# Dilated attention with plain f32 queries and keys, double-buffered loads, and both attentions' first loads moved ahead

## The reference

```python
DIL_GROUPS = ((128, 1), (512, 4), (2048, 16))
for g in range(G):
    idx = t[:, None] - offsets[g][None, :]
    kg, vg = k_groups[g][:, idx], v_groups[g][:, idx]
    logits = jnp.einsum('bqhd,bqkhd->bhqk', qb[:, :, g], kg) * scale + group_bias[g]
    logits = jnp.where(valid, logits, NEG_INF)
    lse = jax.nn.logsumexp(logits, axis=-1)
    outs.append(einsum('bhqk,bqkhd->bqhd', jnp.exp(logits - lse[..., None]), vg)); lses.append(lse)
wts = softmax(stack(lses)); return einsum('gbhq,gbqhd->bqhd', wts, stack(outs))
```

## Time and profile before

| | |
|---|---|
| Runs | 3153.85, 3158.89, 3159.69 us, median 3158.89 |
| Profiled execution | 3164.19 us, of which the span of the trace is 3162.4 us |
| Granted TensorE clock, mean | 0.964 |
| Busy | PE 2896.8 us (92%), PEld 2372.0, DVE 1163.2, ACT 858.4, POOL 923.8 |
| Chain that ended last | PE 81%, DVE 8%, DMA 4%, issue 3%, ACT 2% |
| QK<-y_odds, loads | 128 of 256 KB |
| Packets under 512 bytes | 26211 of 91069 |

### The profile page before, as it was taken

The page is one execution under the profiler, slowest core; times in us unless marked ns, Lnnn a source line. Parts: engine busy times, 40 slices in busy tenths (PEclk is TensorE's granted clock), DMA queues, the critical chain, the costliest instruction groups (busy, mean ns, idle before and its releaser), DMA issues.

```text
span 3162.4 us, 36743 instructions
## 1 busy us (share of the span) xinstructions
PE 2896.8 (92%) x13588; PEld 2372.0 (75%) x13588; DVE 1163.2 (37%) x1849; ACT 858.4 (27%) x1489; POOL 923.8 (29%) x610
## 2 busy tenths in 40 slices
PE   8996888889999999999999975767889999999998
PEld 5785777767888888886788865657668888888867
DVE  3425777414222222225423133467252222222254
ACT  3304766423110001025210024456340000011141
POOL 2330145342333333342233201122413333333332
PEclk9998999999999999999999986879999999999999
DMA  4336432211111111111235267764211111111111
GB/s 153 129 115 180 121 86 68 74 47 34 47 49 50 46 46 46 53 54 54 80 127 215 74 163 137 109 153 114 83 35 47 47 47 52 46 46 46 67 34 73
DMA packets 91069, 257.03 MB, mean 81 GB/s; under 512 B 26211, under 2 KB 29795, under 8 KB 90647
## 3 DMA queue, kind: packets, MB, share of 16 engines
q1 hardware_dynamic: 76008, 199.74, 22.8%
q10 hardware_dynamic: 14944, 55.74, 4.6%
HBM read 207.24 MB, written 52.93 MB: 82 GB/s over the span
## 4 chain that ended last, share of the span: by engine, by line
PE 81%; DVE 8%; DMA 4%; issue 3%; ACT 2%; SPq 1%; POOL 1%; DVEq 0%; ACTq 0%; POOLq 0%
PE ACC L1097 68%; PE ACC L1243 4%; PE OP L1280 3%; PE TR L1257 3%; DMA QK<-y_odds 2%; PE OP L1167 2%; DVE XL L1723 1%; DVE PT L1880 1%; DVE H L1743 1%; DVE T L1740 1%; SPq L725 1%; ACT PT L1517 1%; DVE PB L1863 1%; PE OP L1270 1%; DVE XF L1914 1%
## 5 line engine op out<-in xcount | busy, mean ns | idle before, releaser
L928 POOL CAST WH<-RAW 128x1024 fp32r<-128x1024 f32 x203 | 213.7, 1053 | 1552.2 <-PE ACC L1097 1532.8
L1097 PE MATMUL ACC<-XH,WH 128*128 128x512 f32 x1792 | 574.3, 402 | 47.8 <-DVE XL L1723 27.1
L1097 PE MATMUL ACC<-XL,WH 128*128 128x512 f32 x1792 | 557.1, 392 | 0.0
L1097 PE MATMUL ACC<-XH,WL 128*128 128x512 f32 x1792 | 556.2, 392 | 0.0
L930 POOL TENSOR_TENSOR WL<-RAW,WH 128x1024 fp32r<-128x1024 f32 x203 | 490.5, 2416 | 24.8 <-POOL WH L928 1.5
L1097 PEld LDWEIGHTS ACC<-XH,WH 128*128 128x128 f32 x1792 | 337.4, 189 | 147.1 <-issue 65.4
L1097 PEld LDWEIGHTS ACC<-XL,WH 128*128 128x128 f32 x1792 | 339.7, 190 | 71.9
L1097 PEld LDWEIGHTS ACC<-XH,WL 128*128 128x128 f32 x1792 | 339.2, 189 | 71.8
L1478 ACT ACTIVATE HH<-T 128x1024 fp32r<-128x1024 f32 x64 | 68.0, 1062 | 1149.9 <-DVE T L1765 1149.9
L1772 DVE TENSOR_TENSOR M<-M,ACC 128x1024 f32<-128x1024 f32 x128 | 156.3, 1221 | 482.8 <-PE ACC L1097 480.6
L1097 PE MATMUL ACC<-HH,WH 128*128 128x512 f32 x1024 | 316.7, 390 | 3.3 <-DVE M L1772 3.1
(11 more groups left out here) (197 smaller groups left out, 3288.6 us busy)
## 6 DMA issues: line engine op xcount, KB each, us to landing
RAW<-in_w SPq DMA_DIRECT2D x203, 512.0 KB, 3.4
QK<-y_odds SPq DMA_DIRECT2D x128, 256.0 KB, 6.4
y_odds<-HALVES ACTq DMA_DIRECT2D x16, 1024.0 KB, 5.2
QK<-y_foxs SPq DMA_DIRECT2D x48, 256.0 KB, 5.4
y_foxs<-HALVES ACTq DMA_DIRECT2D x8, 1024.0 KB, 5.1
y_kv<-Q ACTq DMA_DIRECT2D x8, 512.0 KB, 2.6
BIAS<-y_f SPq DMA_DIRECT2D x8, 512.0 KB, 7.0
H<-in_xT ACTq DMA_DIRECT2D x8, 512.0 KB, 7.5
```

The costliest lines, as they stand in the source:

```text
L928: nc.gpsimd.tensor_copy(WH[:, slot], RAW[:, slot]).then_inc(s_whi, 1)
L1097: mm = nc.tensor.matmul(acc[:, h * HALF:(h + 1) * HALF], w(k), x[:, k, h * HALF:(h + 1) * HALF], start=first and k == k0 and w is ws and x ...
```

## The change

Queries and keys of the dilated groups are stored plain (y_odd, 20 tiles; those of the NSA and fox jobs stay split). A dilated job loads queries and keys of both heads as they are into QF (two places, by the job's number modulo 2), with one load of both biases; all its loads are issued by `dilated_loads` as soon as the job before has turned its V and the job two back that used the place is scored. A logit is one plain f32 product over the 64 rows of its head. The minima and sums of a d1 job are turned on PE (32 columns of NML to 32 rows), copied to ZT and stored in pieces of 512 bytes; the merge works on 32 partitions by 32 tokens. CQH and CQL move so that QK is free during up0. SP issues the first fox job's RV and QK before up0's weights, and the first dilated job's RV, QF and BIAS before in1c's weights.

```diff
@@ -69,9 +69,9 @@
-    segs.append(("in1p", 1, [full("odds", 0, 0, "x1"), full("odds", 1, 0, "x1"), full("odd", 6, 0, "x1"),
+    segs.append(("in1p", 1, [full("odd", 8, 0, "x1"), full("odd", 9, 0, "x1"), full("odd", 6, 0, "x1"),
                              full("odd", 7, 0, "x1")]))
-    segs.append(("in1a", 5, [full("odds", c, 2, "x1") for c in (2, 3)]))
+    segs.append(("in1a", 5, [full("odd", 8 + c, 2, "x1") for c in (2, 3)]))
     segs.append(("in1b", 3, [full("odd", c, 2, "x1") for c in (0, 1)]))
@@ -275,13 +275,17 @@
             j.before = jobs[-1] if jobs else None
+            same = [x for x in jobs if x.kind in DILATED and x.slot == j.slot] if kind in DILATED else []
+            j.same, j.loads = same[-1] if same else None, len(same) + 1
+            stacked = [x for x in jobs if x.kind in NSA]
+            j.stacked = stacked[-1] if stacked else None
             jobs.append(j)
@@ -432,8 +438,9 @@
         CQ = sb("CQ", [P, 3, S], 96)
-        CQH = sb("CQH", [P, 3, S], 108, F32R)
-        CQL = sb("CQL", [P, 3, S], 120, F32R)
+        CQH = sb("CQH", [P, 3, S], 0, F32R)
+        CKVL = sb("CKVL", [P, 1, S], 12, F32R)
+        CQL = sb("CQL", [P, 2, S], 16, F32R)
         MISC1 = sb("MISC", [P, 1, S], 132)
@@ -455,6 +462,7 @@
         RK = sb("RK", [P, S], 76)
+        QF = [sb("QF0", [P, 2, S], 8), sb("QF1", [P, 2, S], 180)]
         QK = sb("QK", [P, 2, 4, S], 96, F32R)
@@ -718,39 +739,71 @@
+            def load(dst, src, signal):
+                sp.dma_start(dst, src).then_inc(signal, 16)
+            def head_loads(j, e):
+                y = y_foxs if j.kind == "fox" else y_odds
+                q = y[j.pair + (12 if j.kind in NSA else 0)]
+                for half in range(2):
+                    load(QK[rows_of_head(half), e, 0].bitcast(F32), q[1 - half, rows_of_head(e)], s_head[e])
+                for r in range(2 if j.kind != "cmp" else 0):
+                    for half in range(2):
+                        if j.kind in ("sel", "win"):
+                            src = y[14 if j.kind == "sel" else 15, 1 - half, 0:HD]
+                        else:
+                            src = y[j.pair + (4), 1 - half, rows_of_head(e)]
+                        load(QK[rows_of_head(r), e, 2 + half].bitcast(F32), src, s_head[e])
+            def dilated_loads(j, prior=None):
+                g = j.pair + 2 * DILATED.index(j.kind)
+                if prior:
+                    sp.wait_ge(s_tr, prior.vgroups[-1].tr)
+                load(RV[:], y_odd[g], s_load)
+                if j.same:
+                    sp.wait_ge(s_ttr, j.same.tasks[-1].no + 1)
+                load(QF[j.slot][:, 0], y_odd[8 + g], s_dj[j.slot])
+                load(QF[j.slot][:, 1], y_odd[14 + g], s_dj[j.slot])
+                w = D16_W if j.kind == "d16" else DIL_W
+                load(BIAS[:, :, 256 * j.slot:256 * j.slot + w],
+                     b_tile[j.kind][2 * j.pair:2 * j.pair + 2].rearrange("h p w -> p h w"), s_dj[j.slot])
             def attention(name):
...
-                def load(dst, src, signal):
-                    sp.dma_start(dst, src).then_inc(signal, 16)
                 def sums_out(j):
...
-                    g = DILATED.index(j.kind)
+                    g, c0 = DILATED.index(j.kind), j.tasks[0].col
+                    if j.kind == "d1":
+                        sp.wait_ge(s_zc, j.pair + 1)
+                        sp.dma_start(z_sums[j.pair, g].rearrange("m e (i p) -> (m e i) p", p=P), ZT[:])\
+                            .then_inc(s_zs[g], 16)
+                        return
                     sp.wait_ge(s_exp, j.tasks[-1].no + 1)
...
                         for e in range(2):
-                            c0 = j.tasks[NB * e].col
-                            src, dst = NML[:, m, c0:c0 + NB], z_sums[j.pair, g, m, e]
-                            if j.kind == "d1":
-                                dst = dst.rearrange("(i p) -> p i", p=P)
-                            elif j.kind == "d4":
+                            src, dst = (minima, row_sums)[m](c0 + NB * e, NB), z_sums[j.pair, g, m, e]
+                            if j.kind == "d4":
                                 src = src.rearrange("p (b a) -> p b a", b=2)
...
                                 dst = dst.rearrange("(p i) -> p i", i=NB)
-                            sp.dma_start(dst, src, allow_slow_non_contiguous=j.kind == "d1").then_inc(s_zs[g], 16)
+                            sp.dma_start(dst, src).then_inc(s_zs[g], 16)
@@ -760,6 +813,18 @@
                     before = j.before if j is not ph.jobs[0] else None
+                    if j.kind in DILATED:
+                        if before:
+                            dilated_loads(j, before if before.vgroups else before.before)
+                        if before and before.kind in DILATED:
+                            sums_out(before)
+                        last_bias = j
+                        continue
+                    if j.kind == "mla" and j.pair == 0:
+                        last = tiles[seg_end["up0"] - 1]
+                        sp.wait_ge(s_store[0], 16 * last.store[0])
+                        sp.wait_ge(s_store[1], 16 * last.store[1])
                     if j.vgroups:
@@ -788,22 +851,13 @@
-                        if before:
-                            sp.wait_ge(s_qk, before.tasks[NB * e + NB - 1].no + 1)
-                        g = 2 * DILATED.index(j.kind) if j.kind in DILATED else 0
-                        y = y_foxs if j.kind == "fox" else y_odds
-                        q = y[j.pair + (12 if j.kind in NSA else g)]
-                        for half in range(2):
-                            load(QK[rows_of_head(half), e, 0].bitcast(F32), q[1 - half, rows_of_head(e)], s_head[e])
+                        user = j.stacked if j.kind in NSA else before
+                        if user:
+                            sp.wait_ge(s_qk, user.tasks[NB * e + NB - 1].no + 1)
+                        if before or name != "even":
+                            head_loads(j, e)
                         if j.kind == "cmp":
                             continue
-                        for r in range(2):
-                            for half in range(2):
-                                if j.kind in ("sel", "win"):
-                                    src = y[14 if j.kind == "sel" else 15, 1 - half, 0:HD]
-                                else:
-                                    src = y[j.pair + (4 if j.kind == "fox" else 6 + g), 1 - half, rows_of_head(e)]
-                                load(QK[rows_of_head(r), e, 2 + half].bitcast(F32), src, s_head[e])
@@ -846,17 +900,19 @@
             skew("d16", 8, D16_W)
-            for name in ("in0p", "in0b", "in0c", "up0"):
+            for name in ("in0p", "in0b", "in0c"):
                 weights(name)
...
-            last = tiles[seg_end["up0"] - 1]
-            sp.wait_ge(s_store[0], 16 * last.store[0])
-            sp.wait_ge(s_store[1], 16 * last.store[1])
+            for t in (segs["in0b"].iters[1][0].tiles[0], segs["in0c"].iters[0][0].tiles[0]):
+                sp.wait_ge(s_store[t.pair], 16 * t.store[t.pair])
+            sp.wait_ge(s_x, applies["cq"] + 3)
+            job = phases["even"].jobs[0]
+            load(RV[:], y_fox[0], s_load)
+            for e in range(2):
+                head_loads(job, e)
+            weights("up0")
+            sp.wait_ge(s_tile, segs["up0"].iters[0][1].tiles_end)
             sp.wait_ge(s_misc, 32)
-            sp.wait_ge(s_tile, seg_end["up0"])
-            sp.wait_ge(s_evD, tiles[seg_end["up0"] - 1].dve)
             attention("even")
@@ -881,6 +937,12 @@
             weights("in1b")
+            job = phases["odd"].jobs[0]
+            for t in (segs["in1p"].iters[0][0].tiles[0], segs["in1a"].iters[2][0].tiles[0], segs["in1b"].iters[0][0].tiles[0]):
+                sp.wait_ge(s_store[t.pair], 16 * t.store[t.pair])
+            sp.wait_ge(s_hsp, 16 * DC)
+            sp.wait_ge(s_bd, 16 * 6)
+            dilated_loads(job)
             weights("in1c")
@@ -889,9 +951,6 @@
             sp.wait_ge(s_vst, 32)
-            sp.wait_ge(s_hsp, 16 * DC)
-            sp.wait_ge(s_bd, 16 * 6)
             sp.dma_start(CMPMASK[:], ins["cmpmask"]).then_inc(s_bd, 16)
@@ -1225,6 +1284,14 @@
                     wait(pe, s_ttr, t.acc_free)
+                    if kind in DILATED:
+                        if t.first_of_head and e == 0:
+                            pe.wait_ge(s_dj[t.job.slot], 48 * t.job.loads)
+                        rows = rows_of_head(e)
+                        q, k = (QF[t.job.slot][rows, m, token(kind, b0):token(kind, b0) + c * (n - 1) + 1:c]
+                                for m, b0, n in ((0, t.i, P), (1, t.blocks[0], w)))
+                        nc.tensor.matmul(score_bank(t), q, k, start=True, stop=True).then_inc(s_qk, 1)
+                        return
                     if t.first_of_head and kind == "mla":
@@ -1257,6 +1324,11 @@
                         tr.then_inc(s_tr, 1)
```

(27 more changed lines are left out.)

57 lines of the change are left out of this document (31 added, 26 removed).

## The result

The changed kernel takes 3172.35 us (median of 5 runs, 3166.57 to 3175.32), the kernel before 3155.44 us (5 runs, 3151.96 to 3159.69): ratio 1.0045, 95% interval 1.0031 to 1.0059. It is slower by 17 us; 3094 us was forecast, and the range ended at 3116.

The account below looks back on a forecast made before the run. Late loads were taken to bound the dilated and compressed jobs; elsewhere TensorE's products run back to back. Gains 11 + 12 + 3 + 13 + 18 + 3 + 2 + 3 = 65 us, from 3158.89 to 3094; range 3079 to 3116.

Parts of the forecast that it names:

- Term 6: Dilated logits as one plain f32 product over 64 rows: 3 us gained, from -17 to +14.
- rival (d): Dilated jobs: stride costs f32 nothing, the clock stays up, second d1 start gains 4 us: 3078 us; chance 0.10.
- (a): Dilated logits: f32 passes run in series, 17 us lost instead of 3 gained: 3114 us; chance 0.12.
- (e): Dilated tasks: half-height products do not hold the upper clock, all 96 run at 1.2 GHz, +69 us: 3163; chance 0.02.
- the rows say it hides: Dilated f32 logits: weight loads hide behind the pass before, since four passes with 194 ns loads fit into 0.71 us.
- The 0.69 us: Each d1 task of 256 columns if weight loads do not hide, instead of 0.47; two d1 jobs 6 us more.
- three signs of being wrong: GpSimd waits for RAW in up0, d1 tasks space over 1.1 us, or the clock in the dilated jobs falls.
- Term 1: Start of the even attention: loads moved ahead of up0 bring the first exponential to about 281, 11 us gained (10 to 13).
- Term 2: Start of the odd attention: first exponential at about 1859 instead of 1871.26, 12 us gained (11 to 13).
- Term 3: Inside the dilated jobs: late second-head BIAS and small QK waits go, about 3 us gained.
- Term 4: The two d16 jobs: waits for RV and QK go whole, 13 + 18 us, and 3 us of clock (0 to 6).
- Term 5: Second d1 job: the wait behind the DW loads stays, but fewer bytes follow RV, 2 us gained (1 to 4).

Follow-up runs that it names:

- experiment 3: Changed kernel with dilated logits over all 128 rows and from neighbouring columns, leaving out head separation and token choice: 3081.78 us, ratio 0.9751.
- experiment 1: Changed kernel with each dilated logit product over all 128 rows, both heads' queries and keys, instead of 64: 3102.1 us, ratio 0.9821.
- experiment 5: Changed kernel computing everything, with zeros in the other head's query rows so dilated logits run over 128 rows: 3105.26 us, ratio 0.9826.
- experiment 6: experiment 5 with GpSimd copying d4 and d16 queries and keys into token order, so TensorE reads neighbouring columns: 3087.24 us, ratio 0.9774.
- experiment 2: Changed kernel with dilated logits reading neighbouring columns, still 64 rows, leaving out the choice of tokens: 3165.62 us, ratio 0.9987.
- experiment 8: Kernel before the change, with only the even attention's first 13 loads moved ahead of segment up0: 3151.76 against 3161.25 us, ratio 0.9971.
- experiment 12: experiment 6 with the second d1 job's loads and sel's first V, QK and BIAS ahead of the merge weights: 3076.7 us, ratio 0.9733.
- experiment 13: experiment 12 without the early load of the first d1 job in front of the odd attention: 3088.4 us, ratio 0.9773.
- experiment 10: Changed kernel with two added full-height products of 128 f32 columns ahead of each d1 logit: 3170.08 us, ratio 1.002.

## Why the prediction was wrong

**Term 6 failed, and with it the sign.** "Nearest rows: 384 f32 columns of L1270 take 2001.69 - 2000.98 = 0.71 us ..., 1.85 ns a column, so 256 columns 0.47 us": that row is a product over 128 rows, the new one runs over 64. The row's price is right for its own kind (0.44 and 0.22 us in experiment 3) and wrong here in three parts. (1) A 64-row product does not hide its weight load: 0.2 us for each of 96, and up to 0.15 for the turn behind it; an estimate from these steps is 30 us. (2) With these logits the clock stays at, or falls to, 1.2 GHz in d1 and in part of d16 (0.50 and 0.74); the rest of experiment 1's 70 us, about 40 by the same estimate. (3) The prediction let the stride slow the weight load alone. The columns that stream pay too, 0.44 us per 128 instead of 0.22 even over 128 rows (experiments 1 and 3), so that a strided 256 takes 0.99 us where the old two products took 0.63; the stride costs 18 us in all (experiments 5 and 6; part of it was paid before the change too).

The sum closes: the other terms promised 62 us, so from 3155.44 the kernel should have come to 3093; it came to 3172. If they all came as forecast, term 6 is 79 us lost, where 3 were to be gained and its bounds ended at 17 lost. Rows alone account for 70, rows and stride together for 91. That is 12 more than is missing, about the 11 that rival (d) had put on a stride that costs f32 nothing.

**The rivals.** (a) passes in series, at 0.12, and (e) half-height products that do not hold the upper level, at 0.02, were both partly true at once, and were weighed as if only one could come. (e) came nearest, 3163, and was dismissed because "f32 passes have more columns than they", the compressed tasks. But neither side of that weighing is a row over 64 rows: the compressed logits are full-height products of few columns. The sentence "the rows say it hides" took full-height loads as evidence for half-height ones, while the trace had half-height ones too (1952.02, shown in experiment 2). The 0.69 us that the prediction gives beside it, for loads that don't hide, is nearer to the 0.62 of experiment 2 than its 0.47. Of the prediction's three signs of being wrong all came: the cast in up0 waited for RAW (harmless), a d1 job took 35.1 us for 16 tasks, and the clock fell.

**The other terms.** Term 1, 11 us: 9.2 by experiment 8, 10.2 in the trace (first exponential at 282.07 instead of 292.25). Term 2, 12: 12.6 in the trace, 11.7 by experiments 12 and 13, on a kernel with other logits. Term 3, 3 us: no wait for QF is left, but no run shows what that is worth. Term 4: both waits at d16 are gone, 31 us, which no run measures by itself; its 3 us of clock came out as a loss and belong to part (2). Term 5, 2 us (1 to 4), was too small: 6.48 + 1.33 us wait instead of 8.60 + 4.84, 5.6 less. The first d1 logits, the turned sums and the unsplit tiles left TensorE no wait of their own.

## What to carry to other kernels

Price a product by a row of its own height: halving the rows saved TensorE nothing here, and cost it the hidden weight load and the upper clock level together; rows of zeros cost less than rows left out. This holds for half-height products between full-height ones; half-height ones back to back, on different halves of the array, were not tried. When a change fills idle time with work, look for what the clock does then, not only for the waits that go. When a load is moved ahead of a queue, ask which engine works off what stood in front of it: here the merge on GpSimd became the next thing to wait for, so 7 us of wait gave 3 of time in that job.

## What the runs showed of the hardware

- A busy TensorE can stay at 1.2 GHz: 35.1 us without a gap at a granted clock of 0.50, with products over 64 rows between full-height ones; with full-height work added it went to 0.94 in the same place (experiment 10).
- A product over 64 rows between full-height ones does not hide its weight load: 256 plain f32 columns take 0.62 us at the upper level, over 128 rows 0.44, and rows of zeros do as well as numbers (experiments 2, 3 and 5).
- Strided f32 columns (every 4th or 8th element) take 0.44 us per 128 at the upper level, neighbouring ones 0.22. At the lower level the stride hardly shows: a 128-column logit over 64 rows steps 0.77 us with it (changed kernel, 1926.68) and 0.73 without (experiment 2, 1885.69).
- GpSimd orders 1024 strided f32 columns in 2.07 us, for 128 partitions, and in 2.1 us for 64 (experiment 6).
